# Channel norms with the squares as the stationary operand, and their roots taken per token

## The reference

```python
def _rmsnorm(x, g, eps=NORM_EPS):
    xf = x.astype(jnp.float32)
    y = xf * lax.rsqrt(jnp.mean(xf * xf, axis=-1, keepdims=True) + eps)
    return (y * g.astype(jnp.float32)).astype(x.dtype)

def modulate(x, g, shift, scale):
    return rms_norm(x, g) * (1.0 + scale) + shift
```

## Time and profile before

| what | value |
|---|---|
| median of the runs | 6849.6 us (6817.69 to 6851.7) |
| the profiled execution | 6849.45 us, span 6847.4 us |
| mean granted TensorE clock | 0.874 of 2.4 GHz |
| TensorE busy | 5491.2 us (80%), 22257 matmul passes |
| VectorE busy | 2066.3 us (30%) |
| ScalarE busy | 1309.3 us (19%) |
| GpSimd busy | 729.2 us (11%) |

### The profile page before, as it was taken

One profiled execution on the slowest core, in us unless ns is written; L12 is line 12 of the kernel. 1 busy time (PEld: TensorE's weight loads), 2 busy tenths in 40 slices (PEclk: granted clock), 3 DMA queues, 4 the chain that ended last, 5 costly groups with the idle time before them and its releaser, 6 DMA issues. The chain is left out here.

```text
span 6847.4 us, 59345 instructions
## 1 busy us (share of the span) xinstructions
PE 5491.2 (80%) x22257; PEld 3102.6 (45%) x22257; DVE 2066.3 (30%) x3406; ACT 1309.3 (19%) x2046; POOL 729.2 (11%) x499
## 2 busy tenths in 40 slices
PE   5577677869997598899899357686868888699999
PEld 1266466425443443344344136373646564344444
DVE  7234434126203501211100344343443362211101
ACT  3111112004103500222200111111111241122200
POOL 0022012000000000000000103132221000100000
PEclk9777677889998798999999668787979999899999
DMA  4100000110110011111132000000001000111011
GB/s 73 36 11 1 11 11 1 32 28 1 33 43 28 28 37 50 40 40 37 60 108 66 13 10 4 10 10 3 13 0 26 4 1 25 31 40 37 28 46 49
DMA packets 287249, 191.95 MB, mean 28 GB/s; under 512 B 28823, under 2 KB 264138, under 8 KB 287050
## 3 DMA queue, kind: packets, MB, share of 16 engines
q1 hardware_dynamic: 287050, 189.07, 10.3%
HBM read 175.41 MB, written 13.63 MB: 28 GB/s over the span
## 5 line engine op out<-in xcount | busy, mean ns | idle before, releaser
L570 PE MATMUL psum<-ffn_in,up_slots 128*128 128x512 f32 x2816 | 1214.1, 594 | 65.5 <-DMA up_slots<-in_w_up_dram 41.4
L570 PEld LDWEIGHTS psum<-ffn_in,up_slots 128*128 128x128 f32 x2816 | 537.3, 191 | 742.3 <-issue 742.3
L607 DVE SCALAR_TENSOR_TENSOR conv<-u,conv_cols_a,conv 128x1024 f32<-128x1024 f32 x88 | 113.0, 1284 | 984.8 <-ACT conv L589 984.8
L497 PE MATMUL psum<-x,gate_slots 128*128 128x512 f32 x768 | 340.6, 602 | 30.7 <-DMA gate_slots<-in_w_in_dram 30.7
L442 PE MATMUL psum<-hidden,w_slots 128*128 128x512 f32 x704 | 305.3, 597 | 16.7 <-DMA w_slots<-in_w_down_dram 16.7
L1995 PE MATMUL psum<-hidden,w_slots 128*128 128x512 f32 x704 | 305.8, 596 | 10.9 <-DMA w_slots<-in_ffn_w_down_dram 10.9
L586 ACT ACTIVATE u<-psum 128x512 f32<-128x512 f32 x176 | 105.1, 597 | 894.1 <-PE psum L570 894.1
L497 PEld LDWEIGHTS psum<-x,gate_slots 128*128 128x128 f32 x768 | 148.5, 194 | 218.2 <-issue 186.3
L2478 PE MATMUL psum<-h,w_slots 128*128 128x512 f32 (+1 forms) x576 | 217.6, 540 | 34.9 <-DMA w_slots<-in_w_in_dram 32.6
L621 POOL TENSOR_TENSOR hidden<-conv 128x1024 f32 x44 | 103.1, 2343 | 1327.6 <-DVE conv L611 1327.6
L1459 PE MATMUL psum<-x,w_slots 128*128 128x512 f32 x384 | 173.2, 614 | 72.0 <-DMA w_slots<-in_w_in_dram 72.0
(11 more groups left out here) (532 smaller groups left out, 8608.2 us busy)
## 6 DMA issues: line engine op xcount, KB each, us to landing
mod_slots<-in_w_mod_dram SPq DMA_DIRECT2D x12, 2048.0 KB, 8.3
up_slots<-in_ffn_w_up_dram SPq DMA_DIRECT2D x44, 512.0 KB, 3.8
up_slots<-in_w_up_dram SPq DMA_DIRECT2D x44, 512.0 KB, 3.9
w_slots<-in_w_in_dram SPq DMA_DIRECT2D x33, 512.0 KB, 4.2
gate_slots<-in_w_in_dram SPq DMA_DIRECT2D x24, 512.0 KB, 4.1
w_slots<-in_ffn_w_down_dram SPq DMA_DIRECT2D x8, 1408.0 KB, 12.5
w_slots<-in_w_down_dram SPq DMA_DIRECT2D x8, 1408.0 KB, 7.1
rows_in<-in_x_dram SPq DMA_DIRECT2D x16, 512.0 KB, 3.5
```

Of the source, the lines that this page charges most:

```text
L497: last = nc.tensor.matmul(T.ps[b][:, :], slots[:, s, k, :], rhs[:, k, j * HALF:(j + 1) * HALF], start=(k == 0), stop=(k == kt - 1))
L570: last = nc.tensor.matmul(T.ps[b][:, :], slots[:, q, k, :], h[:, k, j * HALF:(j + 1) * HALF], start=(k == 0), stop=(k == KD - 1))
L607: nc.vector.scalar_tensor_tensor(out=conv[:, q, :], in0=u[:, q, first:first + S], scalar=conv_w[first][:, bass.ds(col, 1)], in1=conv[:, q, :],
```

## The change

The squares become the stationary operand. For each channel tile and each of the eight tiles of 128 tokens, TensorE loads the 128x128 squares and streams one column of ones, which leaves the sums of 128 tokens in one PSUM column, one token per partition. Mean, root and reciprocal are then taken on a 128x8 tile. VectorE copies each token's inverse root along 128 columns, and TensorE multiplies each such tile with the identity, which puts the inverse roots of the 1024 tokens back on all partitions, in PSUM banks 1 and 2. The scaling reads them there. The channel tiles are squared from the last to the first. The block has nine semaphores in place of seven. Apart from that, the order in which the gates sum their channel tiles changes.

```diff
 def channel_rms(nc, T, src, dst, kd, at, n, gain, eps, shift=None):
-    halves = [(c, min(HALF, n - c)) for c in range(0, n, HALF)]
-    with sbuf(nc, "squares", [P, 2, n]) as squares, sbuf(nc, "inv_rms", [P, n]) as inv:
-        with stage(nc, "squared", "summed", "mean_made", "root_made", "inverse_made", "scaled", "shifted") as (
-                block, squared, summed, mean_made, root_made, inverse_made, scaled, shifted):
+    tiles = n // P
+    with sbuf(nc, "squares", [P, 2, n]) as squares, sbuf(nc, "token_stats", [P, 2, tiles]) as stats, sbuf(nc, "wide", [P, tiles, P]) as wide:
+        root, inverse = stats[:, 0, :], stats[:, 1, :]
+        with stage(nc, "squared", "summed", "mean_made", "root_made", "inverse_made", "widened", "spread", "scaled", "shifted") as (
+                block, squared, summed, mean_made, root_made, inverse_made, widened, spread, scaled, shifted):
             @block.scalar
             def _(act):
                 for k in range(kd):
                     if k >= 2:
                         act.wait_ge(summed, k - 1)
-                    nc.scalar.activation(squares[:, k % 2, :], src[:, k, at:at + n], ACT.Square).then_inc(squared, 1)
-                act.wait_ge(mean_made, len(halves))
-                nc.scalar.activation(inv[:, :], inv[:, :], ACT.Sqrt).then_inc(root_made, 1)
+                    nc.scalar.activation(squares[:, k % 2, :], src[:, kd - 1 - k, at:at + n], ACT.Square).then_inc(squared, 1)
+                act.wait_ge(mean_made, 1)
+                nc.scalar.activation(root, root, ACT.Sqrt).then_inc(root_made, 1)
             @block.tensor
             def _(pe):
                 for k in range(kd):
                     pe.wait_ge(squared, k + 1)
-                    for j, (c, w) in enumerate(halves):
-                        last = nc.tensor.matmul(T.ps[j][:, 0:w], T.ones[:, :], squares[:, k % 2, c:c + w],
-                                                start=(k == 0), stop=(k == kd - 1))
+                    for t in range(tiles):
+                        last = nc.tensor.matmul(T.ps[0][:, t:t + 1], squares[:, k % 2, t * P:(t + 1) * P], T.ones[:, 0:1],
+                                                start=(k == 0 and t == 0), stop=(k == kd - 1 and t == tiles - 1))
                     last.then_inc(summed, 1)
+                pe.wait_ge(widened, 1)
+                for t in range(tiles):
+                    last = nc.tensor.matmul(T.ps[1 + t // 4][:, (t % 4) * P:(t % 4 + 1) * P], wide[:, t, :], T.ident[:, :],
+                                            start=True, stop=True)
+                last.then_inc(spread, 1)
             @block.vector
             def _(dve):
                 dve.wait_ge(summed, kd)
-                for j, (c, w) in enumerate(halves):
-                    nc.vector.tensor_scalar(inv[:, c:c + w], T.ps[j][:, 0:w], 1.0 / (kd * P), eps,
-                                            ALU.mult, ALU.add).then_inc(mean_made, 1)
+                nc.vector.tensor_scalar(root, T.ps[0][:, 0:tiles], 1.0 / (kd * P), eps, ALU.mult, ALU.add).then_inc(mean_made, 1)
                 dve.wait_ge(root_made, 1)
-                nc.vector.reciprocal(inv[:, :], inv[:, :]).then_inc(inverse_made, 1)
+                nc.vector.reciprocal(inverse, root).then_inc(inverse_made, 1)
                 dve.wait_ge(inverse_made, 1)
+                nc.vector.tensor_copy(wide[:, :, :], inverse.rearrange("p (t o) -> p t o", o=1).to_broadcast([P, tiles, P])
+                                      ).then_inc(widened, 1)
+                dve.wait_ge(spread, 1)
                 for k in range(kd):
                     nc.vector.scalar_tensor_tensor(out=dst[:, k, at:at + n], in0=src[:, k, at:at + n], scalar=gain[:, k:k + 1],
-                                                   in1=inv[:, :], op0=ALU.mult, op1=ALU.mult).then_inc(scaled, 1)
+                                                   in1=T.psum[:, HALF:HALF + n], op0=ALU.mult, op1=ALU.mult).then_inc(scaled, 1)
...
-GATE_ORDER = (7, 2, 1, 0, 5, 3, 6, 4)
+GATE_ORDER = (7, 0, 5, 3, 4, 1, 2, 6)
```

## The result

The changed kernel takes 6865.5 us, the median of 20 runs (6829.2 to 6877.5), where 20 runs of the kernel before gave 6847.8. The ratio is 1.0023, with a 95% interval from 1.0012 to 1.0034: 8 to 23 us slower. The prediction said 6868.6 us and +19.1.

What follows compares the result with a forecast made beforehand. Seven barrier-ended blocks, one engine at a time on the path, pass gains or losses on in full. +51.5 - 27.3 - 5.9 + 0.8 = +19.1 us on 6849.45 gives 6868.6 us; range 6832 to 6890.

Steps and rivals of the forecast that it cites:

- The sum phase: TensorE's sums of squares in seven blocks: 624 one-column passes at 0.213 us, low clock, 134.3 us against 82.8, +51.5 us.
- (a): Rival for the sums: low-clock loads run at 0.107 us, phases 70.2 us, total 6804 us; chance 0.07.
- The tail: From each sum phase's end to the first scaling: 5.14 us against 9.04, seven times, -27.3 us.
- The small steps: In the tail, mean, root, reciprocal and copy along 128 columns, with hand-offs: 1.39 us, and 0.07 around it.
- the spread: In the tail, 16 passes of 128 columns against the identity: 3.68 us at the low clock.
- GpSimd's shift: In the two calls with a shift, eight shifts take 22.6 us against 25.52: 2.9 us less each, -5.9 us.
- The rest: Remaining effects: +0.8 us for semaphores; reversed tile order and gates' order change no count and wait for nothing.
- The two semaphores: Two more cleared by SyncE ahead of each block's barrier, 0.053 us each, +0.8 us over seven blocks.
- the PSUM operand: The scaling's third operand read from PSUM: taken as no cost, bound +1.8 us.
- the gates' order: New order of eight products in the gates: changes no count, waits for nothing, no cost.
- (b): Rival: the clock rises within the phase as before, phases cost the same, tail 3.4 us, total 6805 us; chance 0.08.
- (c): Rival for one-column passes: each costs the load's whole latency, 0.333 us at the low clock, total 6957 us; chance 0.05.

Runs made afterwards that it cites:

- The one-part experiment: The kernel before with only the reciprocal's 128x1024 result written to PSUM and read there by the scaling; 6841.7 us, ratio 0.9983.

## Why the prediction was right

**The sum phase** was the step that carried the sign. Predicted 134.3 us for 624 passes, measured 6.64 + 3.57 + 4 x 27.46 + 13.51 = 133.6 (-82.8 before: +50.8 for +51.5). Its two halves are now shown separately. The price per load at the two clocks: 3.41 and 1.84 us for the same sixteen passes in one execution. That narrow work leaves the clock low: 0.50 over windows of 26 to 27 us in all four of the changed kernel's eight-tile phases, and a rise within the phase, about 5 us in, when the stream was 128 columns wide. The row that settled the price beforehand was L1691's, loads of the same size at the same clock, and not the faster 36-row transposes, rival (a). Two readings on the way were off and harmless, since no phase ran high. The high price of 0.107 came from start times rounded to 0.1 us and a first gap of 0.03 us; L2127's other gaps are 0.112, and the passes of 128 columns came every 0.112 too. And the sentence that none of the narrow work was granted the high level overlooks these two-column passes: twenty of them ran at 1.00 in 2.29 us right behind wide work, before the clock fell.

**The Trainium skill's figure** ("TensorE: Matmul & The Clock Gate", section "LDWEIGHTS (loading the stationary operand)"), columns over 1.2 GHz, gives an estimate of 107 ns for 128 columns. At the low clock, 1.2 GHz, these fp32 loads came every 213 ns, and every 112 at the high one. So it is near only at 2.4 GHz, and where the clock stays low the measured 213 ns decides.

**The tail** was predicted at 5.14 us and measured between 5.06 and 5.29. The small steps took 1.46 to 1.47 as predicted (1.39 and 0.07), the spread 3.56 to 3.79 for 3.68. Seven times, -26.7 for -27.3.

**GpSimd's shift** was predicted at 22.6 us and took 22.58, twice -2.9. The one-part experiment shows the cause that was only argued before: the inverse root as a second SBUF operand of VectorE's scaling. The Trainium skill's rule ("GPSIMD Engine Reference", section "8. Key points") agrees: 25.52 us with two SBUF inputs, 22.59 with one.

**The rest.** The two semaphores cost 0.11 us per block (0.107 predicted), the PSUM operand nothing (L341 1.275 us in the median), and the gates' order nothing. The sum is +50.8 - 26.7 - 5.9 + 0.8 = +19.0 us; the medians differ by 17.7, with 8 to 23 as the interval. That the sum came within 0.1 us of the +19.1 forecast is in part luck: the phases were put 0.7 us too high and the tails 0.6 too low. No term was off by more than that. Of the 3.1 us between 6868.6 and the median, 1.7 are in the starting point, 6849.45 for a median of 6847.8 over 20 runs.

**The rivals.** (a) and (b) both needed phases of 14 to 16.5 us and got 27.46. (b) did describe a real state, but it took a wider stream to reach it. With 128 columns the phases took 84.5 us for (b)'s 82.8, and the tails 3.56 for its 3.4: 42 us less than before in the blocks for its 44.7. The ratios, 0.9925 and 0.9927, are some 6 us lower still, which the intervals cannot tell. (c), 0.333 us a pass, fell with 0.213: loads recorded at 333 ns each started every 213, so they overlapped even with one column streaming.

**What the prediction missed** is beside its sum. It saw that the load sets the pass and that the clock decides everything. It did not draw the consequence that more columns would cost nothing (sixteen passes of 128 columns took 3.78 us at the low clock, of one column 3.57, the difference being the last one's) and might lift the clock.

## What to carry to other kernels

When a reduction is turned round so that the data is stationary and a single column streams, price it by the load, at the clock that comparable narrow work was granted in the same kernel, and not by the columns it saves. Where the load sets the pace, widen the stream to what hides under it and look at the granted clock again: here 128 columns for one turned +0.23% into -0.75%. And where GpSimd works beside VectorE, see whether one of VectorE's two SBUF operands can live in PSUM: here it took GpSimd's eight shifts from 25.52 to 22.59 us and VectorE's scalings from 12.16 to 9.62.

## What the runs showed of the hardware that was not expected

The same program with the same call can be granted either clock. In the kernel with added wide work, two of four identical eight-tile phases stayed at 0.50, for 55.0 us each, and two went from 0.50 to 1.00 within their first 8 us and took 31.4 and 31.9.

Whole executions differ by steps for the same kind of reason. L1645 of the kernel before (L1648 in the others named here, a 64x256 product of the RWKV part, not touched by any edit), by line and shape, in the profiled executions of before, of after (the first measurement of the version with 128 columns has the same row), and of the second measurement of that version, in this order:

```profile
L1645 PE MATMUL psum<-kt_rt,bt_kd 64*128 64x256 f32 x128 | 58.7, 560 | 6.0 <-PEq L51 6.0
```

```profile
L1648 PE MATMUL psum<-kt_rt,bt_kd 64*128 64x256 f32 x128 | 51.9, 501 | 6.0 <-PEq L51 6.0
```

```profile
L1648 PE MATMUL psum<-kt_rt,bt_kd 64*128 64x256 f32 x128 | 58.7, 560 | 6.0 <-PEq L51 6.0
```

It is 58.7 us or 51.9, and the line behind it 58.7 or 51.6: 14 of the 16.5 us by which the profiled execution of after was ahead at its first norm. The stretch comes four times in an execution. Windows inside the third time, of before and then of after:

```profile
833.00:863.00 30.00, 30.00 (x91) 24.93 (x92) 12.64 (x33) 0.00 (x0) 11.27 (x9) 0.52 0.00 1
```

```profile
832.00:847.00 15.00, 15.00 (x87) 13.44 (x87) 11.99 (x31) 0.00 (x0) 10.06 (x9) 1.00 0.00 1
```

The same stretch took 31.0 us in the one (0.52) and 16.4 in the other (1.00), so the step is the granted clock of one such stretch. The two measurements of the version with 128 columns are one program, and their profiled spans are 6780.9 and 6802.3 us. A single pair of profiled executions can therefore hide or feign a change of this size (19 us). From first square to first scaling the same block of that program came within 0.4 us in both.
